# A hybrid convolution and sparse-attention layer: head outputs moved to the other half of the partitions by DMA and added on GpSimd, with other order tables and another opening

## What is computed

```python
h = rmsnorm(x, norm_in) * (1.0 + scale) + shift          # shift, scale, gate from silu(c) @ w_ada
proj = h @ w_in                                          # 4680 columns, split in 11 parts
y_conv = group_rmsnorm(short_conv_mixer(cb, cc, cu, conv_w, conv_b), ...) * silu(cz)
score = sum over 8 index heads of w_idx * relu(q_idx . k_idx), causal; sel = top 256 keys of each query
p = softmax(q . k over the selected keys); y_attn = p @ v    # 8 heads of 64
y_attn = group_rmsnorm(y_attn, gn_attn, N_HEADS) * silu(az)
y = concatenate([y_conv, y_attn]) @ w_out
return rmsnorm(x + gate * y, norm_f)
```

## Time and profile before

| | us |
|---|---|
| median of 3 runs (lowest to highest) | 691.47 (690.11 to 692.19) |
| the profiled execution | 691.02 |
| its span, first to last instruction | 689.2 |
| PE busy in it | 653.6 (95%) |
| DVE, ACT, POOL busy in it | 449.9, 376.2, 228.2 |

### The profile page before, as it was taken

How to read it: one execution, slowest core, us unless ns; L and a number is a source line. 1 busy time by engine, 2 the same in 40 slices (tenths; PEclk the granted TensorE clock), 3 DMA queues, 4 the chain that set the end, 5 groups by cost and what they waited for, 6 DMA issues and landing times.

```text
span 689.2 us, 8964 instructions
## 1 busy us (share of the span) xinstructions
PE 653.6 (95%) x3203; PEld 546.5 (79%) x3203; DVE 449.9 (65%) x750; ACT 376.2 (55%) x546; POOL 228.2 (33%) x121
## 2 busy tenths in 40 slices
PE   0899999999999999999999999999999999999996
PEld 0789987878888888888888887887877877778884
DVE  5784635767889999895049660004889898577625
ACT  6765435656662233453643354435889989874302
POOL 1001215343334152666645776440036432000000
PEclk9999999999999999999999999999999999999999
DMA  8960497453333010101010451053974550222431
GB/s 320 380 225 1 119 167 179 131 153 93 92 91 123 31 61 31 61 31 62 30 62 31 135 202 61 32 117 67 308 181 93 124 123 29 96 91 94 152 122 61
DMA packets 27911, 78.64 MB, mean 114 GB/s; under 512 B 3986, under 2 KB 8410, under 8 KB 27868
## 3 DMA queue, kind: packets, MB, share of 16 engines
q1 hardware_dynamic: 27524, 77.03, 37.6%
q10 hardware_dynamic: 344, 1.05, 0.6%
HBM read 61.25 MB, written 13.41 MB: 108 GB/s over the span
## 4 chain that ended last, share of the span: by engine, by line
PE 85%; DVE 4%; SPq 3%; DMA 3%; ACT 2%; issue 2%; POOL 1%; DVEq 0%; ACTq 0%; POOLq 0%
PE ps L802 17%; PE ps L803 17%; PE ps L804 17%; PE ps L1010 4%; PE ps L1011 4%; PE ps L1012 4%; PE ps L837 4%; PE ps L870 3%; PE ps L871 2%; PE ps L958 2%; PE ps L957 2%; PE ps L890 2%; PE ps L889 2%; DMA raw<-in_w_units 2%; SPq L558 1%
## 5 line engine op out<-in xcount | busy, mean ns | idle before, releaser
L802 PE MATMUL ps<-hH,wH 128*128 128x512 f32 (+1 forms) x544 | 211.8, 389 | 1.8 <-issue 1.7
L804 PE MATMUL ps<-hH,wL 128*128 128x512 f32 (+1 forms) x544 | 210.1, 386 | 0.0
L803 PE MATMUL ps<-hL,wH 128*128 128x512 f32 (+1 forms) x544 | 210.1, 386 | 0.0
L1841 POOL TENSOR_TENSOR wL<-raw,wH 128x1024 fp32r<-128x1024 f32 x35 | 86.7, 2476 | 184.7 <-ACT wH L1064 176.3
L802 PEld LDWEIGHTS ps<-hH,wH 128*128 128x128 f32 x544 | 102.1, 188 | 22.4 <-issue 3.8
L804 PEld LDWEIGHTS ps<-hH,wL 128*128 128x128 f32 x544 | 102.1, 188 | 20.4
L803 PEld LDWEIGHTS ps<-hL,wH 128*128 128x128 f32 x544 | 102.2, 188 | 18.3
L1265 ACT ACTIVATE relu<-ps,wabs 128x384 f32<-128x384 f32 (+5 forms) x48 | 40.0, 850 | 39.7 <-PE ps L890 18.7
L1567 DVE SCALAR_TENSOR_TENSOR score<-relu,wsgn,score 128x384 f32<-128x384 f32 (+5 forms) x42 | 49.7, 1184 | 13.8 <-ACT relu L1265 10.9
L1588 DVE TENSOR_SCALAR_CACHE_REDUCE above<-score,srch 128x384 bf16<-128x384 f32 (+5 forms) x60 | 56.8, 946 | 2.1
L1683 DVE TENSOR_TENSOR phL<-ps,phH 128x512 fp32r<-128x512 f32 (+1 forms) x80 | 49.5, 633 | 11.0 <-ACT phH L1223 10.1
(11 more groups left out here) (232 smaller groups left out, 1176.7 us busy)
## 6 DMA issues: line engine op xcount, KB each, us to landing
raw<-in_w_units SPq DMA_DIRECT2D x36, 512.0 KB, 3.4
ks<-qk_halves SPq DMA_DIRECT2D x32, 256.0 KB, 5.9
xin<-in_x SPq DMA_DIRECT2D x8, 512.0 KB, 7.5
wa<-in_w_ada SPq DMA_DIRECT2D x8, 512.0 KB, 11.9
wa<-in_w_ada SPq DMA_DIRECT2D x16, 256.0 KB, 7.5
gw<-in_w_ada SPq DMA_DIRECT2D x8, 512.0 KB, 4.1
qs<-qk_halves SPq DMA_DIRECT2D x16, 256.0 KB, 4.2
wo<-in_w_out SPq DMA_DIRECT2D x8, 512.0 KB, 7.6
```

The costliest lines, as they stand in the source:

```text
L802: pe.matmul(out, wH[slot(n)][:, kt, :], hH[:, kt, cols], start=(kt == 0), stop=False)
L803: pe.matmul(out, wH[slot(n)][:, kt, :], hL[:, kt, cols], start=False, stop=False)
L804: mm = pe.matmul(out, wL[slot(n)][:, kt, :], hH[:, kt, cols], start=False, stop=(kt == KT - 1))
L1841: g.tensor_tensor(wL[slot(n)][:], raw[slot(n)][:], wH[slot(n)][:].bitcast(F32), ALU.subtract).then_inc(s_wL, 1)
```

## The change

**Head outputs.** For the first seven heads (`SHIFTED` = 14 halves) ScalarE copies the whole bank, all 128 partitions, in one instruction: for even heads into `ya`, for odd heads into one new buffer `obuf`. SP then moves the 64 wanted partitions by a DMA to `tmp` on the other 64 (`shift_out`), and GpSimd adds them into `ya` (`join`, semaphore `s_join`). PE waits for the ScalarE copy (`s_tmp`) where it waited for the VectorE sum. The last head is as before. `shift_out(2h-1)` stands on SP's queue ahead of the loads of head h+2, `shift_out(2h)` behind them. The 6 loads of `w_out` are spread over two places, and GpSimd splits slice 3 after the third pair of heads.

**Tables.** LOGITS_AT, MAX_AT, EXP_AT, the place of the copy, and those of denominators and sums are other numbers; PE's denominators move from place 13 to 9 of a head, block 5's logits from 14 or 15 to 16.

**Opening.** Parts 6 and 7 of the first `w_ada` group change places on SP. ScalarE makes `hH` straight from the source, ahead of `xT`, both by an Identity activation; the high part of unit 2's weights comes after slice 0. PE's unit 1 waits for `xT` 0, unit 2 for `xT` 1 as before. The load for unit 7 is issued together with that of unit 6.

```diff
-LOGITS_AT = (1, 3, 10, 13, 14, 15, 16, 18)
-MAX_AT = (1, 2, 9, 14, 14, 15, 15, 18)
-EXP_AT = (9, 13, 13, 16, 16, 17, 19, 21)
+LOGITS_AT = (2, 5, 5, 11, 16, 16, 18, 20)
+MAX_AT = (0, 4, 6, 10, 15, 16, 17, 20)
+EXP_AT = (6, 9, 15, 18, 18, 19, 21, 24)
-TMP_AT, OUT_AT = 5, 5
+TMP_AT, OUT_AT = 4, 5
+SHIFTED = 2 * (NH - 1)
...
-DENS_AT = {HEAD * (2 * t + 1) + (13 if t < NT - 1 else 7): t for t in range(NT)}
+DENS_AT = {HEAD * (2 * t + 1) + (9 if t < NT - 1 else 7): t for t in range(NT)}
...
+        obuf = at("obuf", [P, HALF], F32, 12)
...
+        def out_read(engine, g):
+
+            if g < SHIFTED:
+                engine.wait_ge(s_tmp, g + 1)
+            else:
+                engine.wait_ge(s_o, g - SHIFTED + 1)
...
-                for i, dst in enumerate(wa[g]):
+                for i in (tuple(range(KT - 2)) + (KT - 1, KT - 2) if g == 0 else range(len(wa[g]))):
+                    dst = wa[g][i]
...
-                if NSLOT <= n < NU - 2 and n != LOAD_EARLY:
+                if NSLOT <= n < NU - 2 and n not in (NSLOT + 1, LOAD_EARLY):
                     load(n + 2)
+                if n == NSLOT:
+                    load(n + 3)
...
+            def shift_out(g):
+
+                sp.wait_ge(s_tmp, g + 1)
+                if g:
+                    sp.wait_ge(s_join, g)
+                r, d = rows(g // 2), rows(g // 2 + 1)
+                sp.dma_start(tmp[r, :], kept_out(g)[d, :]).then_inc(s_shift, 16)
+
+            load_head(0)
+            load_head(1)
+            for h in range(NH):
+                if h:
+                    shift_out(2 * h - 1)
+                if h + 2 < NH:
+                    load_head(h + 2)
+                if h < NH - 1:
+                    shift_out(2 * h)
...
-                        if n == 2:
-                            pe.wait_ge(s_h, 2)
+                        if n:
+                            pe.wait_ge(s_h, n)
...
-                    pe.wait_ge(s_o, 2 * h + 1 if at_step > 5 else 2 * h - 1)
+                    out_read(pe, 2 * h if at_step > 5 else 2 * h - 2)
...
-            split_high(2)
...
+                A(hH[:, kt, :], src, ACT.Identity, bias=shift[:, kt:kt + 1], scale=amp[:, kt:kt + 1]).then_inc(s_hH, 1)
                 A(xT[:, kt, :], src, ACT.Identity, bias=shift[:, kt:kt + 1], scale=amp[:, kt:kt + 1]).then_inc(s_h, 1)
-                act.wait_ge(s_h, kt + 1)
-                A(hH[:, kt, :], xT[:, kt, :], ACT.Copy).then_inc(s_hH, 1)
                 if kt == 0:
+                    split_high(2)
...
-                if g >= 1:
-                    act.wait_ge(s_o, g)
-                A(tmp[r, :], ps[d, 6 + sb, :], ACT.Copy).then_inc(s_tmp, 1)
+                if g < SHIFTED:
+                    if h % 2 and g > 2:
+                        act.wait_ge(s_join, g if sb else g - 2)
+                    A(kept_out(g), ps[:, 6 + sb, :], ACT.Copy).then_inc(s_tmp, 1)
...
-                    if x in OUTS:
+                    if x in OUTS and OUTS[x] >= SHIFTED:
                         head_out(OUTS[x])
...
+            def join(g_):
+
+                h, sb = g_ // 2, g_ % 2
+                r = rows(h)
+                pool.wait_ge(s_shift, 16 * (g_ + 1))
...
+                g.tensor_tensor(ya[r, h // 2, HALF * sb:HALF * sb + HALF], kept_out(g_)[r, :], tmp[r, :],
+                                ALU.add).then_inc(s_join, 1)
```

More of the change, by code:

```diff
@@ L638, in spread_den, with load_head @@
                                  dd[t, NB * e:NB * e + NB, :].rearrange("(o b) n -> o (b n)", o=1).broadcast_to([HD, S])).then_inc(s_din, 16)
-            for h in range(NH):
+            def load_head(h):
                 if h == 2:
@@ L649, in _ @@
                                      dqk[min(i, 1), part, h, :, :]).then_inc(s_stack[h % 2], 16)
-                if h == 2:
-                    for ct in range(KT - 2):
-                        sp.dma_start(wo[:, ct, :], a["w_out"][P * ct:P * ct + P, :]).then_inc(s_wo, 16)
-                if h >= 3 and h % 2:
-                    spread_den((h - 3) // 2)
+            def shift_out(g):
[13 more added lines that the diff above has]
+                    shift_out(2 * h)
+                    if h < 2:
+                        for ct in range(3 * h, 3 * h + 3):
+                            sp.dma_start(wo[:, ct, :], a["w_out"][P * ct:P * ct + P, :]).then_inc(s_wo, 16)
+                    if h % 2:
+                        spread_den(h // 2)
             sp.wait_ge(s_exp, NB * NH)
@@ L1904, in _ @@
                     mm.then_inc(s_vv, 1)
-            def pair_square(t, half):
-                pool.wait_ge(s_o, 4 * t + half + 3)
+            def join(g_):
+                h, sb = g_ // 2, g_ % 2
+                r = rows(h)
+                pool.wait_ge(s_shift, 16 * (g_ + 1))
+                if g_ % 4 == 3:
+                    pool.wait_ge(s_ygP, g_ // 2)
+                elif g_ % 4 == 2:
+                    pool.wait_ge(s_join, g_)
+                elif g_ % 4 == 0 and g_:
+                    pool.wait_ge(s_ygP, g_ // 2)
+                elif g_ == 1:
+                    pool.wait_ge(s_join, 1)
+                elif g_ % 4 == 1:
+                    pool.wait_ge(s_woL, g_ // 4 + 1)
+                g.tensor_tensor(ya[r, h // 2, HALF * sb:HALF * sb + HALF], kept_out(g_)[r, :], tmp[r, :],
+                                ALU.add).then_inc(s_join, 1)
+            def pair_square(t, half):
+                if t < NT - 1:
+                    pool.wait_ge(s_join, 4 * t + half + 3)
+                else:
+                    pool.wait_ge(s_join, 4 * t + half + 1)
+                    pool.wait_ge(s_o, half + 1)
                 if t or half:
@@ L1927, in pair_add @@
                 pool.wait_ge(s_sums, 2 * t + half + 1)
+                if half == 0:
+                    pool.wait_ge(s_join, 4 * t + 5)
                 pool.wait_ge(s_din, 32 * (t + 1))
```

38 lines of the change are left out of this document (27 added, 11 removed).

## The result

| us | before | after |
|---|---|---|
| median (runs) | 691.55 (6) | 695.68 (6) |
| lowest to highest | 690.11 to 692.19 | 694.51 to 696.94 |
| ratio, 95% interval | | 1.0066 (1.0052 to 1.0080) |
| span of the profiled execution | 689.2 | 693.6 |
| PE busy, DVE busy, POOL busy in it | 653.6, 449.9, 228.2 | 656.1, 448.9, 247.8 |

What follows compares the result with a forecast made beforehand. PE was taken as the bound, busy 653.6 of 689.2 us. From the profiled 691.02, opening +0.6, unit 7 -1.6 and attention -2.6 (-3.7 and +1.1) gave 687.4, plus 0.45 for the median 687.9 us; range 684.5 to 692.8.

Steps and rivals of the forecast that it cites:

- Opening: Kernel's start: slice 1's `xT` later delays PE's unit 2 by 1.0 us, a vanished `hH` wait returns 0.4; net +0.6 us.
- Unit 7: PE's 1.57 us wait at 106.89 us: the load issued some 10 us earlier removes it, -1.6 us.
- rival 4: Unit 7's hole only moves, to the index scores or the next unit: 689.5 us, chance 0.10.
- Engine work: Attention: VectorE loses 9.6 us of sums, GpSimd gains 18.1 us, ScalarE's copies add nothing.
- No cost of the port: Attention: GpSimd's 14 sums beside VectorE's low parts were taken to cost nothing through the shared port.
- the sign named in the prediction: Listed under attention's signs: VectorE's busy time down by about 9.6 us, GpSimd's up by about 18.
- PE's old waits: Attention: waits for `dT` (-2.5) and `ya` (-0.4) go, those for `phL` halve (-0.8); sum -3.7 us.
- The bound of -5.2: Attention's largest possible gain: PE's idle time in the middle stretch, scaled to attention's 119 us.
- The widest block: Attention: its logits, maximum, exponential and first chunk's turn stand closer, 0 to 3.5 us over seven heads, taken as +1.1.
- The late half's path: Attention: first half's copy, shift behind key loads and join leave some 3.5 us at the median landing; cost 0.
- Rival 1: Join too late at odd heads, delaying ScalarE's second-half copy at heads 1, 3 and 5: 695.4 us, chance 0.13.

## Why the prediction was wrong, point by point

**Opening** (+0.6). The factors came at 29.77 instead of 30.0, slice 1's `xT` ended at 36.25 instead of 36.8, unit 2 began at 36.39 instead of 36.9: +0.45 there, where +1.0 was forecast. That delay is right in kind; the net is not, for the units began 0.3 us earlier instead of 0.6 later. In the time it is 0 (1.0005, 0.9996 to 1.0014).

**Unit 7** (-1.6). Wrong, and as rival 4 said. I had written that the index queries' transfers now stand behind 512 KB more, and had only let PE's scores wait for them. They are first waited for by ScalarE's copy of the next queries, and unit 6's high part stands behind it. The index scores got a wait of 1.1 us on top. The term measured 0 (1.0006, 0.9990 to 1.0021).

**Engine work.** VectorE's head sums fell by 9.5 us as forecast, GpSimd rose by 19.6 (18.1 forecast). ScalarE's copy of 128 x 512 took 0.59. No cost of the port on `phL` (median 682 ns, before 686). But the sign named in the prediction, VectorE's busy time down by about 9.6, did not come: it fell by 1.0 us over the span (449.9 to 448.9). In attention it fell by 6.3 (102.2 to 95.9), and ahead of attention it rose by 5.4. Single operations took longer there: two `T<-T,swap` 6.6 us instead of 4.5, seven sums of `gacc` 17.2 instead of 15.2, the first score 2.6 instead of 0.9. In attention it was `dsq`, with two SBUF inputs: four small ones took 1.8 us in all instead of 0.65, one of them 1.32. No experiment took this apart, and "no cost from the port" is shown for `phL` alone.

**PE's old waits** (-3.7). All gone, 4.6 us, and 4.8 with `azs`. The `phL` waits went in full, not by half. The bound of -5.2 was scaled up from the middle stretch (and its own figure was 5.1); read over the whole of attention, PE's idle time before was 122.40 - 115.40 = 7.0 us:

```profile
479.60:602.00 122.40, 115.40 (x703) 96.82 (x702) 102.17 (x222) 110.12 (x229) 36.17 (x27) 1.00 0.51 134
```

**The widest block** (+1.1). It measured 0.8 us, at one place.

**The late half's path** (0). This is the step that failed. I reckoned the first half's shift, behind the key loads, against ScalarE's next copy, found 3.5 us of room, and wrote "the same for the squares and group sums behind the joins, whose room is smaller, about 1 us". The second half's shift I never followed on SP. The diff puts `spread_den` at the end of the odd head's turn, directly ahead of `shift_out(2h+1)`; it issues one DMA and then waits for its landing. "SP gains 14 issues, beside nothing that PE waits for directly" is the sentence that passed over it. Before, only the next head's loads stood behind that wait, and it was short. The landings of `den_rows` before and after:

```profile
DMA to landing us min/median/max: 1.3/1.3/2.0
DMA to landing us min/median/max: 1.6/5.2/7.7
```

So SP's wait got longer and got an urgent transfer behind it at once. The term was 4.9 us of waiting and 1.7 of clock, 3.6 of the 4.9 at this place; most of the rest, 1.07, was the second pair's, whose join stood 2.7 us behind its data. In the sum for the first half, six issues took 3.8 us (514.51 to 518.29) and not 2.6.

**Rival 1** gave 695.4 and the side that came out. That it is so near 695.68 is luck, for its place was another: ScalarE was not the one that waited, and no load landed later than 9 us after its issue. A shift that landed in 3.8 us had been issued 2.7 us late, and PE waited for its squares directly. With that wait and one split of w_out moved, attention is 2.1 us shorter than before in the fastest trace, where 2.6 was forecast; in the median nothing of it is left (1.0004, 0.9992 to 1.0016).

**The range** reached to 692.8. It had left out rival 1 with 0.13, and no term in it for the clock, though PE's idle time was redistributed in every part of it.

## What to carry to other kernels

A queue that issues for several consumers is only as early as its one instruction that waits for a landing: when transfers are added to it, list what stands behind each such wait, not only what stands ahead of the new transfer. A hole that is closed by starting a transfer earlier can be paid by the transfers that now stand behind it: here a hole of 1.6 us became one of 1.4 a unit earlier, so look at the neighbouring places before counting the gain. Parts of a change can need each other: here the tables alone (1.0040) and the shifts with the old tables (1.0128) both lost, and together they were level with the kernel before only once a wait on a queue that no table covers was moved too (1.0004).

## What the runs showed of the hardware

In four traces PE had a hole of 3.4 to 4.5 us, and the granted clock was then 0.50, the 1.2 GHz level, for 3.4 us in three of them and 6.8 in one. In the changed kernel's first trace it fell 1.2 us after PE had started again (the rows of 521 to 525 are full of matmuls); in its second it fell 0.7 us before the hole's end. Matmuls of 512 columns start 0.43 us apart in the stretch (522.24 to 522.67 for one pair) and 0.23 apart at full clock, so in a kernel whose PE is 95% busy a hole of 3.6 us cost 1.7 more, half as much again as it shows in the list of waits. The Trainium skill, page "TensorE: Matmul & The Clock Gate", section "Part 1: The HAM clock gate (the "warmup" mystery)", has the clock set by how busy the engine has recently been; the long holes agree (four of four), and behind the short hole at 481 the clock fell only sometimes (four of fifteen). The mean clock of single executions, 0.988 to 0.999 for the same program, and the spans go together: 42 executions of the kernel before at 0.998 or more have a median span of 688.45 us, 28 at 0.996 one of 689.8.
